# The MLP of a hybrid decoder step: seven products with fewer sums, accumulated onto read PSUM banks, and a reordered end

## The chip, the cores and the metric

The kernel runs on one core of a Trainium2 chip, in one launch. The metric is the time of one execution on the device, in microseconds (us). TensorE multiplies, VectorE and ScalarE read PSUM and work on SBUF, GpSimd works on SBUF alone, SyncE issues most of the transfers.

## The reference

One layer for 1024 prompt tokens and 32 sample tokens (T = 1056 rows together, processed side by side) and a model width of 1024. Two attention branches, merged by gates, come first. The change lies behind them:

```python
def finish_layer(x, o_a, o_b, ga, gb, p_emb, w_oa, w_ob, w_o, g_ffn, w_up, w_down, g_ple, w_ple_gate, w_ple):
    ...
    x = x + (jax.nn.sigmoid(ga) * ya + jax.nn.sigmoid(gb) * yb) @ w_o
    x = x + jnp.square(jax.nn.relu(rms_norm(x, g_ffn) @ w_up)) @ w_down
    x = x + jax.nn.sigmoid(rms_norm(x, g_ple) @ w_ple_gate) * (p_emb @ w_ple)
    return x
```

with `w_up` 1024 x 4096, `w_down` 4096 x 1024, `w_ple_gate` 1024 x 1024, `w_ple` 256 x 1024, all in float32. A final RMSNorm follows.

## The kernel before

**Number format.** Every float32 operand is split into a high half (rounded to the format that TensorE takes at full rate, `fp32r`) and a low half, the difference. A product is made of three matmuls, high x high, high x low and low x high. ScalarE makes high halves by a copy, GpSimd or VectorE the low halves by a subtraction. All activations stand transposed, features on partitions, tokens in columns.

**Stages.** `run_tail` is the part that the change touches. One program per engine is written out by hand; the engines meet at semaphores only, and each works in its own order. First the merge of the branches, then the output projection (`out`, 8 units of 128 output features in 3 chunks of 352 columns), whose results VectorE adds to the residual `x_res` (`take_output_unit`, L2494) and squares for the RMSNorm. Then the MLP, then the gates of the per-layer embedding (`ple`), then the final norm and the output.

**The MLP.** It has NP = 16 iterations of 256 hidden features each. The up projection of an iteration is a 2 x 2 block product: weights w11, w12, w21, w22 (128 features by 512 inputs each) and the residual in four quadrants (512 inputs by 528 columns). Seven products stand for the eight (a Strassen scheme). Their right operands, sums of quadrants of x, are made once in the head (`k_sum`, `k_hi`, `k_lo`, token 0 to 6). Their left operands are made in each iteration: SyncE loads raw quadrants, GpSimd multiplies them by the norm's gain (`scale_quad`), VectorE adds two (`sum_entry`, L2698), ScalarE makes the high half (`high_entry`, L2688), GpSimd the low half (`low_entry`, L2671). There are three slots for such an entry (`e_hi`, `e_lo`, `e_sum` share room); an entry may be written once the product three entries back is done (`wait_slot`). The products m2, m3, m6, m1, m5, m7, m4 (`multiply_product`, L2776 to L2778, 24 matmuls of 264 columns each) go to two PSUM banks each by `BANKS`.
The four results c11 to c22 are put together in SBUF: ScalarE copies the first summand out of PSUM (`first_of`, L2996), VectorE adds the others (`take_back`, L2913) and applies relu and the norm's factor (`finish_quad`, L2881), ScalarE squares and rounds (`square`, L3001 and L3005), VectorE makes the low half (`low_quad`, L2894). They are the hidden activations `a`.
The down projection of the iteration before, d0 to d3 (`multiply_down`, L2801 to L2803, 36 matmuls of 352 columns each, six chunks of six, in banks 4 to 7 by turns), stands between m3 and m6 of iterations 1 to 14. VectorE adds each chunk to `x_res` (`add_down`, L2903), and a chunk may start once the chunk four back is added. The last two down projections, of iterations 14 and 15, follow the last product m4 one after the other.

**The head and the end.** For i = 0 the squares of `x_res` are summed over features (`sum_features`, L3217), GpSimd makes the root, VectorE a diagonal (`make_factors`), TensorE spreads it over the partitions (`spread_products`, L3209), VectorE copies the factors `rstd_bc`. During the last down projection VectorE sums squares again (L2987), ScalarE and GpSimd make the halves `h3` of `x_res` (L3060, L2753). Then `embed_unit`: for unit 0 all gate chunks (L661 to L663), with the sums and factors in between, then the embedding products (L3185 to L3187); for units 1 to 7 by turns. The gate weights are gained and split by GpSimd (`split_ple`, L2759 to L2763), and so are the low halves of `w_ple` (`w_ple_lo`, L2391); VectorE makes `p_lo` (L2444).

## Time and profile before

| | |
|---|---|
| median of 3 runs | 2596.54 us |
| lowest and highest | 1940.65 and 3026.96 us |
| profiled execution | 1940.81 us |
| its span, first to last instruction | 1939.1 us |
| mean granted TensorE clock | 0.99 of full |
| busy: TensorE, VectorE, GpSimd, ScalarE | 95%, 57%, 38%, 34% |

The profile shows one execution, whose time is that of the shortest of the three runs. PE is TensorE, DVE VectorE, ACT ScalarE, POOL GpSimd. In the timeline a row has its start in us, its duration, and in brackets the idle time of the engine before it with what ended that; matmuls overlap, so that the distance of two starts is the cost of one. PEclk is the clock that was granted, as a share of full speed.

### The profile page before, as it was taken

Reading aid. Unit: us, or ns where it says so; the run is one execution under the profiler, and the core shown is the slowest. Engines: PE = TensorE matmul, PEld = TensorE weight load, DVE = VectorE, ACT = ScalarE, POOL = GpSimd, SP = SyncE. Lnnn points to the kernel's source line nnn. Section 1 sums busy time; section 2 is a strip of 40 time slices with the busy share of each in tenths; the row PEclk is TensorE's granted clock in tenths of the full one; section 3 lists DMA queues with packets and bytes.
Section 4 is the critical chain, followed back from the end, with each engine's and each line's share of the span. In section 5 each row is a group of like instructions: output and inputs, shape, how many; then the busy total and the mean of one; then the engine's idle time right before and its main releaser. Section 6 shows DMA issues by size and latency. Waiting matters only on the chain.

```text
span 1939.1 us, 35110 instructions
## 1 busy us (share of the span) xinstructions
PE 1848.8 (95%) x13805; PEld 1704.5 (88%) x13805; DVE 1108.3 (57%) x2198; ACT 652.7 (34%) x1274; POOL 739.8 (38%) x581
## 2 busy tenths in 40 slices
PE   8999999999899998999998899999999999988897
PEld 7977799998766666789998899999999999988897
DVE  5144122223848874875456766666666666677665
ACT  5232123323544444651123323333322222245122
POOL 5323122231514010106565544444444444448641
PEclk9999999999999999999999999999999999999999
DMA  7333285651011127016412222222222322222102
GB/s 237 107 121 129 97 246 172 186 165 56 12 43 44 41 59 221 17 44 201 134 44 82 87 88 96 89 88 88 93 98 94 129 98 88 93 71 93 33 23 90
DMA packets 170268, 193.84 MB, mean 100 GB/s; under 512 B 17530, under 2 KB 142298, under 8 KB 169474
## 3 DMA queue, kind: packets, MB, share of 16 engines
q1 hardware_dynamic: 152866, 161.85, 26.4%
q10 hardware_dynamic: 14816, 28.12, 4.1%
q8 instruction: 105, 1.72, 0.4%
q0 software_dynamic: 2432, 1.74, 0.4%
q14 instruction: 49, 0.40, 0.1%
HBM read 161.13 MB, written 63.97 MB: 116 GB/s over the span
## 4 chain that ended last, share of the span: by engine, by line
PE 45%; DVE 4%; POOL 3%; issue 2%; ACT 1%; DMA 0%; DVEq 0%; ACTq 0%; POOLq 0%
PE bank L2801 6%; PE bank L2802 6%; PE bank L2803 6%; PE bank L661 4%; PE bank L662 4%; PE bank L663 4%; PE bank L2776 4%; PE bank L2778 4%; PE bank L2777 4%; DVE c L2881 1%; POOL e_lo L2671 1%; DVE e_sum L2698 1%; DVE c L2913 1%; ACT e_hi L2688 1%; PE bank L3256 0%
## 5 line engine op out<-in xcount | busy, mean ns | idle before, releaser
L2903 DVE TENSOR_TENSOR x_res<-bank,x_res 128x352 f32<-128x352 f32 x384 | 200.7, 523 | 145.6 <-PE bank L2803 145.5
L2776 PE MATMUL bank<-k_hi,e_hi 128*128 128x264 f32 x896 | 260.3, 291 | 19.5 <-POOL e_lo L2671 16.6
L2777 PE MATMUL bank<-k_lo,e_hi 128*128 128x264 f32 x896 | 256.5, 286 | 0.0
L2778 PE MATMUL bank<-k_hi,e_lo 128*128 128x264 f32 x896 | 256.2, 286 | 0.0
L2801 PE MATMUL bank<-a_hi,e_hi 128*128 128x352 f32 x768 | 249.8, 325 | 3.0 <-DVE x_res L2903 3.0
L2802 PE MATMUL bank<-a_lo,e_hi 128*128 128x352 f32 x768 | 247.2, 322 | 0.0
L2803 PE MATMUL bank<-a_hi,e_lo 128*128 128x352 f32 x768 | 247.2, 322 | 0.0
L2671 POOL TENSOR_TENSOR e_lo<-e_sum,e_hi 128x512 fp32r<-128x512 f32 x80 | 112.5, 1407 | 267.9 <-ACT e_hi L2688 267.9
L2776 PEld LDWEIGHTS bank<-k_hi,e_hi 128*128 128x128 f32 x896 | 170.6, 190 | 24.5 <-issue 17.8
L2671 POOL TENSOR_TENSOR e_lo<-raw,e_hi 128x512 fp32r<-128x512 f32 x96 | 143.0, 1496 | 115.3 <-ACT e_hi L2688 113.8
L2778 PEld LDWEIGHTS bank<-k_hi,e_lo 128*128 128x128 f32 x896 | 170.8, 191 | 0.0
L2777 PEld LDWEIGHTS bank<-k_lo,e_hi 128*128 128x128 f32 x896 | 170.7, 190 | 0.0
L2688 ACT ACTIVATE e_hi<-e_sum 128x512 fp32r<-128x512 f32 x80 | 50.7, 634 | 338.7 <-DVE e_sum L2698 338.7
L2801 PEld LDWEIGHTS bank<-a_hi,e_hi 128*128 128x128 f32 x768 | 144.2, 188 | 6.3 <-DVE x_res L2903 5.7
L2803 PEld LDWEIGHTS bank<-a_hi,e_lo 128*128 128x128 f32 x768 | 144.4, 188 | 0.0
L2802 PEld LDWEIGHTS bank<-a_lo,e_hi 128*128 128x128 f32 x768 | 144.3, 188 | 0.0
L974 DVE TENSOR_TENSOR gt_scaled<-bank,rstd_bc 128x352 f32<-128x352 f32 x48 | 25.1, 524 | 195.7 <-PE bank L663 192.5
L449 PE MATMUL bank<-wn_hi,h_hi 128*128 128x512 f32 (+5 forms) x360 | 132.9, 369 | 0.0
L451 PE MATMUL bank<-wn_hi,h_lo 128*128 128x512 f32 (+5 forms) x360 | 131.0, 364 | 0.0
L450 PE MATMUL bank<-wn_lo,h_hi 128*128 128x512 f32 (+5 forms) x360 | 130.5, 363 | 0.0
L2913 DVE TENSOR_TENSOR c<-c,bank 128x528 f32<-128x528 f32 x128 | 89.7, 701 | 69.3 <-PE bank L2778 33.3
L661 PE MATMUL bank<-h_hi,wu_hi_gates 128*128 128x352 f32 x384 | 128.0, 333 | 0.3 <-PEq L314 0.3
(371 smaller groups left out, 4494.0 us busy)
## 6 DMA issues: line engine op xcount, KB each, us to landing
raw<-in_w_up SPq DMA_DIRECT2D x64, 256.0 KB, 3.2
raw<-in_w_down SPq DMA_DIRECT2D x64, 256.0 KB, 2.6
gate_d<-gate_out ACTq DMA_DIRECT2D x16, 528.0 KB, 3.7
f_gates<-gate_d ACTq DMA_DIRECT2D x24, 352.0 KB, 3.9
w_stage_gates<-in_w_in SPq DMA_DIRECT2D x16, 512.0 KB, 6.9
ws_ring<-in_cache_win_k SPq DMA_DIRECT2D x8, 1024.0 KB, 6.0
ws_ring<-in_cache_win_v SPq DMA_DIRECT2D x8, 1024.0 KB, 6.5
ls_keys<-in_cache_ckv SPq DMA_DIRECT2D x64, 128.0 KB, 2.3
```

Source lines behind the costliest of these rows:

```text
L449: pe.matmul(out, a, w, start=k == 0, stop=False)
L450: pe.matmul(out, a, v, start=False, stop=False)
L451: last = pe.matmul(out, c, w, start=False, stop=k == KD - 1)
L661: pe.matmul(out, w, a, start=n == 0, stop=False)
L2671: pool.tensor_tensor(g.e_lo[s][:, :], src[:, :], g.e_hi[s][:, :].bitcast(F32), ALU.subtract).then_inc(g.e_ready, 1)
L2776: pe.matmul(out, w[:, k], a, start=k == 0, stop=False)
L2777: pe.matmul(out, w[:, k], b, start=False, stop=False)
L2778: last = pe.matmul(out, v[:, k], a, start=False, stop=k == 3)
L2801: pe.matmul(out, w[:, k, unit], a_hi[:, k, cols], start=k == 0, stop=False)
L2802: pe.matmul(out, w[:, k, unit], a_lo[:, k, cols], start=False, stop=False)
L2803: last = pe.matmul(out, v[:, k, unit], a_hi[:, k, cols], start=False, stop=k == 1)
L2903: dve.tensor_tensor(x, g.bank[:, 4 + n % 4, :CH], x, ALU.add).then_inc(g.x_added, 1)
```

## The change

The seven products become those of the variant with fewer sums (Winograd's form), p1 to p7. Four weight sums t1 to t4 are made instead of five, t1, t3 and t4 in place over raw quadrants, t2 in the slot of p6. Products whose results are only ever wanted as a sum are accumulated in PSUM: p6 onto p1's banks, after ScalarE has copied these (c11), then p7 onto the same (after the copy for c21), then p4 (after VectorE's take for c22); p3 onto p5's banks. c12 is finished straight from the banks. In iteration 0 some sums stay in SBUF. The order of products is one list, `ORDER`. In the last iteration d0 stands between p2 and p6; the remaining down products of the last two projections alternate.
In the output projection ScalarE makes the high half of the weights (`high_of_weights`) and GpSimd the low half, where GpSimd made both. Four weight quadrants of iteration 0 and two of iteration 1 are gained by ScalarE (`gain_first`). The loads of `w_ple` and `p_t` are issued right behind the last p4 and those of the gate weights behind the last low quadrant; `w_ple_lo` and `p_lo` are made among the last down products. Unit 0 of the embedding starts with its embedding products, then six of eight parts of its gates, the column sums, and the other two parts.

```diff
 CW = HALF // 2
 NP = FF // (2 * P)
 Q = 4 * P
-SUMS = {"m2": 1, "m6": 2, "m1": 3, "m5": 4, "m7": 5}
-PRODUCTS = ("m2", "m3", "m6", "m1", "m5", "m7", "m4")
+PRODUCTS = ("p1", "p2", "p6", "p5", "p7", "p3", "p4")
 DOWN = ("d0", "d1", "d2", "d3")
-TOKENS = {"m2": 0, "m3": 1, "m6": 2, "m1": 3, "m5": 4, "m7": 5, "m4": 6}
-BANKS = {"m2": 0, "m3": 2, "m6": 0, "m1": 4, "m5": 6, "m7": 0, "m4": 2}
-QUADS = ("c22", "c12", "c11", "c21")
-FIRST = ("c21", "c22", "c12", "c11")
-def entries_of(i):
+TOKENS = {"p1": 0, "p7": 1, "p6": 2, "p3": 3, "p5": 4, "p2": 5, "p4": 6}
+LAST = NP - 1
+C_NAMES = ("c11", "c12", "c21", "c22")
+QUADS = {True: ("c22", "c21", "c12", "c11"), False: ("c11", "c22", "c21", "c12")}
+COPIES = {True: ("c11", "c12", "c21", "c22"), False: ("c11", "c21", "c22")}
+TAKES = {True: ("c21+p3", "c22+p7", "c22+x", "c22f", "c21+p5", "c21f", "c12+x", "c12f", "c11+p2", "c11f"),
+         False: ("c11+p2", "c11f", "c22+x", "c22f", "c21+z", "c21f", "c12f")}
+SUMS = {True: ("t3", "t1", "t2", "t4"), False: ("t1", "t2", "t3", "t4")}
+def program_of_products():
+    order = [(0, name) for name in ("p1", "p7", "p6", "p3", "p5", "p4", "p2")]
+    for i in range(1, LAST):
+        order += [(i, name) for name in PRODUCTS[:2] + DOWN + PRODUCTS[2:]]
+    order += [(LAST, name) for name in PRODUCTS[:2] + ("d0",) + PRODUCTS[2:]]
+    return order + [(LAST, "d1"), (NP, "d0"), (LAST, "d2"), (NP, "d1"), (LAST, "d3"), (NP, "d2"), (NP, "d3")]
...
+def bank_of(i, name):
     if i == 0:
...
+        return {"p1": 0, "p6": 0, "p4": 0, "p7": 2, "p3": 6, "p5": 4, "p2": 6}[name]
+    x = 2 * (i % 2)
+    return {"p1": x, "p6": x, "p7": x, "p4": x, "p2": 2 - x, "p5": 4, "p3": 4}[name]
...
+def sum_weights(dve, g, i, name):
+    product = g.e_sum[slot_of(i, "p6")][:, :]
+    if name == "t1":
+        wait_gained(dve, g, i, "w11")
+        wait_gained(dve, g, i, "w21")
+        if i == 0:
+            dve.wait_ge(g.summed, sums_until(0, "t3"))
+        out, one, other = quad_of(g, i, "w21"), quad_of(g, i, "w21"), quad_of(g, i, "w11")
+    elif name == "t2":
+        wait_gained(dve, g, i, "w22")
+        dve.wait_ge(g.summed, sums_until(i, "t1"))
+        wait_slot(dve, g, i, "p6")
+        out, one, other = product, quad_of(g, i, "w22"), quad_of(g, i, "w21")
+    elif name == "t3" and i == 0:
+        wait_gained(dve, g, i, "w21")
+        wait_gained(dve, g, i, "w22")
+        dve.wait_ge(g.w_split, g.out_step.unit + KD)
+        out, one, other = g.raw[2][:, :], quad_of(g, i, "w22"), quad_of(g, i, "w21")
+    elif name == "t3":
+        dve.wait_ge(g.summed, sums_until(i, "t2"))
+        dve.wait_ge(g.e_ready, ENTRY[i, "p1"] + 1)
+        out, one, other = quad_of(g, i, "w11"), product, quad_of(g, i, "w11")
+    else:
+        wait_gained(dve, g, i, "w12")
+        dve.wait_ge(g.summed, sums_until(i, "t2"))
+        if i:
+            dve.wait_ge(g.e_ready, ENTRY[i, "p2"] + 1)
+        out, one, other = g.raw[3][:, :] if i == 0 else quad_of(g, i, "w12"), quad_of(g, i, "w12"), product
+    dve.tensor_tensor(out, one, other, ALU.subtract).then_inc(g.summed, 1)
...
 def split_last(pool, g, stage, split, at):
-    pool.wait_ge(g.w_loaded[0], (g.steps[-1].turn + 1) * 16)
-    pool.wait_ge(g.e_ready, ENTRY[NP - 1, "m4"] + 1)
-    split_ple(pool, g, stage, split, 0, at + 1)
-    for name in DOWN[:3]:
-        low_entry(pool, g, NP, name)
+    low_entry(pool, g, LAST, "d1")
+    low_entry(pool, g, NP, "d0")
+    pool.wait_ge(g.p_hi_s, 1)
+    for n in range(8):
+        part = (slice(None), n // 4, slice(n % 4 * 256, n % 4 * 256 + 256))
+        done = pool.tensor_tensor(g.wp_lo[part], g.wp[part], g.wp_hi[part].bitcast(F32), ALU.subtract)
+    done.then_inc(g.wp_lo_s, 1)
+    low_entry(pool, g, LAST, "d2")
+    low_entry(pool, g, NP, "d1")
     for n in range(NCH * KD):
         if n == 6:
+            low_entry(pool, g, LAST, "d3")
+            low_entry(pool, g, NP, "d2")
+        if n == 12:
             low_entry(pool, g, NP, "d3")
+            pool.wait_ge(g.w_loaded[0], (g.steps[-1].turn + 1) * 16)
+            split_ple(pool, g, stage, split, 0, at + 1)
         m, c = divmod(n, NCH)
         cols = slice(c * CH, (c + 1) * CH)
         pool.wait_ge(g.h3_hi_s, n + 1)
...
+    s, n, bank = slot_of(i, name), TOKENS[name], bank_of(i, name)
+    onto = name in ("p6", "p4") or (i > 0 and name in ("p7", "p3"))
     w, v = (x[s][:, :].rearrange("p (k c) -> p k c", k=4) for x in (g.e_hi, g.e_lo))
     pe.wait_ge(g.e_ready, ENTRY[i, name] + 1)
     for c in range(2):
         out, cols = g.bank[:, bank + c, :CW], slice(c * CW, (c + 1) * CW)
         for k in range(4):
             a, b = g.k_hi[n][:, k, cols], g.k_lo[n][:, k, cols]
-            pe.matmul(out, w[:, k], a, start=k == 0, stop=False)
-            pe.matmul(out, w[:, k], b, start=False, stop=False)
-            last = pe.matmul(out, v[:, k], a, start=False, stop=k == 3)
+            pe.matmul(out, w[:, k], a, start=k == 0 and not onto, stop=False, skip_group_check=onto)
+            pe.matmul(out, w[:, k], b, start=False, stop=False, skip_group_check=onto)
+            last = pe.matmul(out, v[:, k], a, start=False, stop=k == 3, skip_group_check=onto)
     last.then_inc(g.m_done, 1)
...
+def take(dve, g, i, label):
+    at, name = takes_until(i, label), label[:3]
     c = g.c[name][:, :]
-    dve.wait_ge(g.c_s, 12 * i + at - 1)
-    if i == 0:
-        dve.wait_ge(g.bc_got, 3)
-    dve.scalar_tensor_tensor(c, c, 0.0, g.rstd_bc[:, th * HALF:(th + 1) * HALF], ALU.max, ALU.mult).then_inc(g.c_s, 1)
+    t = int(name[2]) - 1
+    rstd = g.rstd_bc[:, t * HALF:(t + 1) * HALF]
+    if label[3] == "f":
+        if i > 0 and name == "c12":
+            dve.wait_ge(g.m_done, DONE[i, "p4"])
+            dve.wait_ge(g.a_lo_s, quads_until(i - 1, name))
+            dve.scalar_tensor_tensor(halved(c), halves_of(g, bank_of(i, "p4")), 0.0, halved(rstd), ALU.max, ALU.mult).then_inc(g.taken, 1)
+            return
+        dve.wait_ge(g.taken, at - 1)
+        if i == 0:
+            dve.wait_ge(g.bc_got, 3)
+        dve.scalar_tensor_tensor(c, c, 0.0, rstd, ALU.max, ALU.mult).then_inc(g.taken, 1)
+        return
+    product = {"x": {"c12": "p4", "c22": "p6" if i == 0 else "p7"}.get(name), "z": "p3"}.get(label[4:], label[4:])
+    dve.wait_ge(g.m_done, DONE[i, product])
+    dve.wait_ge(g.copied_c, copies_until(i, name))
+    dve.wait_ge(g.taken, at - 1)
+    dve.tensor_tensor(halved(c), halved(c), halves_of(g, bank_of(i, product)), ALU.add).then_inc(g.taken, 1)
...
 def accumulate_mlp(dve, g):
-    def last_quads(i):
-        take_back(dve, g, i, "c11", 2, "m4", 9)
-        finish_quad(dve, g, i, "c11", 10)
-        take_back(dve, g, i, "c21", 2, "m4", 11)
-        finish_quad(dve, g, i, "c21", 12)
-        low_quad(dve, g, i, "c11")
+    low_of_last(dve, g, 2)
+    add_square(dve, g, g.rstd_bc, NCH - 1, NCH * KD)
+    low_of_last(dve, g, 3)
+    low_of_both(dve, g, 1)
+    sum_weights(dve, g, 0, "t4")
+    low_of_both(dve, g, 2)
+    low_of_both(dve, g, 3)
+    copy_feature_sums(dve, g)
+    low_late(dve, g, 6, 0, g.late_lo_dve)
+    low_late(dve, g, 6, 1, g.late_lo_dve)
+    make_factors(dve, g, 0)
...
+    for i in range(1, NP):
+        take(dve, g, i, "c11+p2")
+        take(dve, g, i, "c11f")
+        if i < LAST:
+            add_down(dve, g, i, "d0")
+            sum_weights(dve, g, i, "t1")
+            add_down(dve, g, i, "d1")
+            add_down(dve, g, i, "d2", (0,))
+        else:
+            add_down(dve, g, i, "d0", (0, 1))
+            sum_weights(dve, g, i, "t1")
+        for name in ("t2", "t3", "t4"):
+            sum_weights(dve, g, i, name)
+        if i < LAST:
+            add_down(dve, g, i, "d2", range(1, 6))
+            add_down(dve, g, i, "d3")
+            low_quad(dve, g, i, "c11")
+        else:
+            add_down(dve, g, i, "d0", range(2, 6))
+        take(dve, g, i, "c22+x")
+        take(dve, g, i, "c22f")
+        if i == LAST:
+            low_quad(dve, g, i, "c11")
+        low_quad(dve, g, i, "c22")
+        take(dve, g, i, "c21+z")
+        take(dve, g, i, "c21f")
+        take(dve, g, i, "c12f")
         low_quad(dve, g, i, "c21")
...
     dve.memset(g.rstd_bc[:, :], 0.0).then_inc(g.clear_s, 1)
     dve.memset(g.stat[:, :], float(D)).then_inc(g.stat_s, 1)
-    add_down(dve, g, NP - 1, range(24))
+    add_down(dve, g, LAST, "d1")
     dve.wait_ge(g.clear_s, 2)
     for n in range(NCH * KD):
-        add_down(dve, g, NP, (n,))
-        if n:
+        if n == 6:
+            add_last_square(dve, g, n - 1)
+            dve.wait_ge(g.p_hi_s, 2)
+            dve.tensor_tensor(g.p_lo[:, :, :], g.p_t[:, :, :], g.p_hi[:, :, :].bitcast(F32), ALU.subtract).then_inc(g.p_lo_s, 1)
+            add_down(dve, g, LAST, "d2")
+        if n == 12:
+            add_last_square(dve, g, n - 1)
+            add_down(dve, g, LAST, "d3")
+        add_down(dve, g, NP, f"d{n // 6}", (n % 6,))
+        if n not in (0, 6, 12):
             add_last_square(dve, g, n - 1)
     add_last_square(dve, g, NCH * KD - 1)
...
-    pe.wait_ge(g.w_split, st.unit + m + 1)
     if m == 0:
-        for c in range(NCH):
-            gate(c)
         pe.wait_ge(g.wp_lo_s, 1)
         pe.wait_ge(g.p_lo_s, 1)
         for c in range(NCH):
             embedding(c)
+        pe.wait_ge(g.w_split, st.unit + 1)
+        for c in range(NCH):
+            if c == 2:
+                pe.wait_ge(g.x_added, ENDS_OF_CHUNKS)
+            gate(c, range(6))
+        pe.wait_ge(g.acc_s, 2 * NCH * KD)
+        sum_features(pe, g, g.rstd_bc, 7)
+        for c in range(NCH):
+            gate(c, range(6, KD))
+        spread_products(pe, g, 1, 2, CH)
     else:
+        pe.wait_ge(g.w_split, st.unit + m + 1)
         for c in range(NCH):
             gate(c)
             embedding(c)
```

VectorE in a middle iteration, from the finish of c22 to that of c21, which is the last but for two low halves; before:

```order
L2881 SCALAR_TENSOR_TENSOR c22_12599<-c22_12599,rstd_bc_53 128x528
L2913 TENSOR_TENSOR c12_12597<-c12_12597,bank 128x528
L2881 SCALAR_TENSOR_TENSOR c12_12597<-c12_12597,rstd_bc_53 128x528
L2913 TENSOR_TENSOR c11_12596<-c11_12596,bank 128x528
L2698 TENSOR_TENSOR e_sum1_12611<-raw0_12601,raw1_12602 128x512
L2913 TENSOR_TENSOR c11_12596<-c11_12596,bank 128x528
L2894 TENSOR_TENSOR a_lo_12593<-c22_12599,a_hi_12592 128x528
L2894 TENSOR_TENSOR a_lo_12593<-c12_12597,a_hi_12592 128x528
L2913 TENSOR_TENSOR c11_12596<-c11_12596,bank 128x528
L2881 SCALAR_TENSOR_TENSOR c11_12596<-c11_12596,rstd_bc_53 128x528
L2913 TENSOR_TENSOR c21_12598<-c21_12598,bank 128x528
L2881 SCALAR_TENSOR_TENSOR c21_12598<-c21_12598,rstd_bc_53 128x528
```

and of the changed kernel, from the low half of c11 to the end of the iteration:

```order
L3056 TENSOR_TENSOR a_lo_12593<-c11_12596,a_hi_12592 128x528
L3044 TENSOR_TENSOR c22_12599<-c22_12599,bank 128x528
L3038 SCALAR_TENSOR_TENSOR c22_12599<-c22_12599,rstd_bc_53 128x528
L3056 TENSOR_TENSOR a_lo_12593<-c22_12599,a_hi_12592 128x528
L3044 TENSOR_TENSOR c21_12598<-c21_12598,bank 128x528
L3038 SCALAR_TENSOR_TENSOR c21_12598<-c21_12598,rstd_bc_53 128x528
L3033 SCALAR_TENSOR_TENSOR c12_12597<-bank,rstd_bc_53 128x528
L3056 TENSOR_TENSOR a_lo_12593<-c21_12598,a_hi_12592 128x528
L3056 TENSOR_TENSOR a_lo_12593<-c12_12597,a_hi_12592 128x528
```

The takes of c12 and c11 and the weight sum between them are gone from here, c12 is finished from the bank, and the low half of c22 stands ahead of the take of c21.

GpSimd from the last entries of the down products to the first gate units (`e_lo` are entries, `h3_lo` low halves of the residual, `f_stat` the root); before:

```order
L2671 TENSOR_TENSOR e_lo1_12612<-raw4_12605,e_hi1_12610 128x512
L2759 TENSOR_TENSOR w_stage_ple_12627<-w_stage_ple_12627,gains_52 128x1024
L2761 TENSOR_TENSOR wu_ple_12629<-w_stage_ple_12627,ones_50 128x1024
L2763 TENSOR_TENSOR wu_ple_12629<-w_stage_ple_12627,wu_ple_12629 128x1024
L2671 TENSOR_TENSOR e_lo2_12615<-raw5_12606,e_hi2_12613 128x512
L2671 TENSOR_TENSOR e_lo0_12609<-raw4_12605,e_hi0_12607 128x512
L2671 TENSOR_TENSOR e_lo1_12612<-raw5_12606,e_hi1_12610 128x512
L2753 TENSOR_TENSOR h3_lo_12617<-x_res_12630,h3_hi_12616 128x352 x6
L2671 TENSOR_TENSOR e_lo2_12615<-raw4_12605,e_hi2_12613 128x512
L2753 TENSOR_TENSOR h3_lo_12617<-x_res_12630,h3_hi_12616 128x352 x18
L236 TENSOR_SCALAR f_stat_12565<-f_stat_12565 128x9
L239 TENSOR_TENSOR f_stat_12565<-f_stat_12565,nhalf_51 128x9
```

and of the changed kernel:

```order
L2889 TENSOR_TENSOR w_ple_lo_12623<-w_ple_sb_12622,w_ple_hi_12621 128x256 x8
L2853 TENSOR_TENSOR e_lo1_12612<-raw0_12601,e_hi1_12610 128x512
L2853 TENSOR_TENSOR e_lo2_12615<-raw3_12604,e_hi2_12613 128x512
L2904 TENSOR_TENSOR h3_lo_12617<-x_res_12630,h3_hi_12616 128x352 x6
L2853 TENSOR_TENSOR e_lo0_12609<-raw1_12602,e_hi0_12607 128x512
L2853 TENSOR_TENSOR e_lo1_12612<-raw4_12605,e_hi1_12610 128x512
L2904 TENSOR_TENSOR h3_lo_12617<-x_res_12630,h3_hi_12616 128x352 x6
L2853 TENSOR_TENSOR e_lo2_12615<-raw5_12606,e_hi2_12613 128x512
L2910 TENSOR_TENSOR w_stage_ple_12627<-w_stage_ple_12627,gains_52 128x1024
L2912 TENSOR_TENSOR wu_ple_12629<-w_stage_ple_12627,ones_50 128x1024
L2914 TENSOR_TENSOR wu_ple_12629<-w_stage_ple_12627,wu_ple_12629 128x1024
L2904 TENSOR_TENSOR h3_lo_12617<-x_res_12630,h3_hi_12616 128x352 x12
```

The eight pieces of `w_ple_lo` moved from behind the root to ahead of all `h3_lo`, the split of the first gate unit from ahead of the last projection's entries to ahead of the last twelve `h3_lo`.

## Rows read from the trace of the kernel before

**Rows 1.** The page's busy times (busy us, share of the span, instructions).
```profile
PE 1848.8 (95%) x13805; PEld 1704.5 (88%) x13805; DVE 1108.3 (57%) x2198; ACT 652.7 (34%) x1274; POOL 739.8 (38%) x581
```
**Rows 2.** Stretches of 50 us: busy time of each engine, granted clock, DMA.
```profile
1050.00:1100.00 50.00, 38.46 (x269) 37.41 (x270) 37.32 (x40) 20.36 (x29) 31.29 (x17) 0.93 0.10 32
...
1200.00:1250.00 50.00, 49.54 (x351) 49.26 (x350) 32.22 (x53) 14.34 (x24) 21.06 (x16) 1.00 0.26 87
...
1700.00:1750.00 50.00, 43.76 (x316) 43.04 (x315) 35.27 (x51) 18.65 (x31) 20.02 (x16) 0.97 0.23 72
```
**Rows 3.** TensorE's timeline in the loop (start, us, instruction, idle before it).
```profile
1131.70 0.36 PE L2776 MATMUL bank<-k_hi,e_hi 128*128 128x264 f32 x1 [0.45 <-POOL e_lo L2671]
...
1669.53 0.39 PE L2801 MATMUL bank<-a_hi,e_hi 128*128 128x352 f32 x1
...
1692.56 0.28 PE L2776 MATMUL bank<-k_hi,e_hi 128*128 128x264 f32 x1
...
1707.02 0.28 PE L2778 MATMUL bank<-k_hi,e_lo 128*128 128x264 f32 x1
...
1707.74 0.36 PE L2776 MATMUL bank<-k_hi,e_hi 128*128 128x264 f32 x1 [0.45 <-POOL e_lo L2671]
```
**Rows 4.** TensorE's timeline in the head, from the first product.
```profile
1046.49 0.36 PE L2776 MATMUL bank<-k_hi,e_hi 128*128 128x264 f32 x1 [0.60 <-DVE x_res L2494]
...
1060.78 2.02 PE L3209 MATMUL bank<-f_diag,ones 128*128 128x128 f32 x16 [2.17 <-DVE f_diag L3234]
...
1076.19 0.56 PE L2776 MATMUL bank<-k_hi,e_hi 128*128 128x264 f32 x1 [3.86 <-POOL e_lo L2671]
...
1093.44 0.40 PE L2801 MATMUL bank<-a_hi,e_hi 128*128 128x352 f32 x1
```
**Rows 5.** TensorE's timeline in the last iteration, down products and gates.
```profile
1716.77 0.36 PE L2776 MATMUL bank<-k_hi,e_hi 128*128 128x264 f32 x1 [2.81 <-POOL e_lo L2671]
...
1732.95 0.32 PE L2801 MATMUL bank<-a_hi,e_hi 128*128 128x352 f32 x1
...
1739.92 0.43 PE L2801 MATMUL bank<-a_hi,e_hi 128*128 128x352 f32 x1 [2.98 <-DVE x_res L2903]
...
1789.88 0.63 PE L661 MATMUL bank<-h_hi,wu_ple 128*128 128x352 f32 x1 [5.04 <-issue]
...
1815.12 0.43 PE L661 MATMUL bank<-h_hi,wu_ple 128*128 128x352 f32 x1 [3.59 <-POOL wu_ple L2763]
...
1919.79 2.10 PE L3217 MATMUL bank<-ones,final_total 128*128 128x1 f32 x18 [2.67 <-DVE final_total L3162]
```
**Rows 6.** Stretch of 6 us in the head, columns as in rows 2.
```profile
1066.00:1072.00 6.00, 6.00 (x40) 6.00 (x39) 5.87 (x4) 0.07 (x1) 5.85 (x2) 0.74 0.15 44
```
**Rows 7.** VectorE, ScalarE, GpSimd: groups by shape (busy, mean ns), and single rows.
```profile
L2903 DVE TENSOR_TENSOR x_res<-bank,x_res 128x352 f32<-128x352 f32 x384 | 200.7, 523 | 145.6 <-PE bank L2803 145.5
...
L2913 DVE TENSOR_TENSOR c<-c,bank 128x528 f32<-128x528 f32 x128 | 89.7, 701 | 69.3 <-PE bank L2778 33.3 <-ACT c L2996 31.5
...
L2881 DVE SCALAR_TENSOR_TENSOR c<-c,rstd_bc 128x528 f32<-128x528 f32 x64 | 69.5, 1085 | 2.2
...
L2987 DVE TENSOR_TENSOR rstd_bc<-rstd_bc,h_square 128x352 f32<-128x352 f32 x24 | 20.2, 843 | 0.3 <-ACT h_square L3063 0.2
...
L2688 ACT ACTIVATE e_hi<-e_sum 128x512 fp32r<-128x512 f32 x80 | 50.7, 634 | 338.7 <-DVE e_sum L2698 338.7
...
L2671 POOL TENSOR_TENSOR e_lo<-e_sum,e_hi 128x512 fp32r<-128x512 f32 x80 | 112.5, 1407 | 267.9 <-ACT e_hi L2688 267.9
...
L2763 POOL TENSOR_TENSOR wu_ple<-w_stage_ple,wu_ple 128x1024 fp32r<-128x1024 f32 x8 | 19.5, 2436 | 0.6
...
1717.65 1.75 DVE L2698 TENSOR_TENSOR e_sum<-raw,raw 128x512 f32<-128x512 f32 x1 [2.90 <-POOL raw L2654]
...
1801.44 2.89 DVE L2444 TENSOR_TENSOR p_lo<-p_t_sb,p_hi 128x2112 fp32r<-128x2112 f32 x1
...
1824.72 0.53 DVE L3162 TENSOR_TENSOR final_total<-final_total,tail_square 128x352 f32<-128x352 f32 x1 [0.57 <-ACT tail_square L2481]
```

793 lines of the change are left out of this document (421 added, 372 removed).

## The prediction

> **What bounds the kernel now.** I read the page's busy shares first. TensorE is busy for 1848.8 us of a span of 1939.1 [rows 1], so only the time in which it stands, or runs at half clock, can be won. The stretches of 50 us [rows 2] say where: from 1100 to 1700 us it is saturated (49.5 of 50), and just ahead of that and from 1700 on it loses 6 to 12 us in a stretch. The change touches the program from the output projection (from about 950 us) to the end. So I then read TensorE's own timeline there, stage by stage: what ended each wait, and how long a stage takes beside its bare matmul work.
>
> The bare work comes from one full iteration of the MLP loop. Its four down products (144 matmuls of 352 columns) run from 1669.53 to 1692.56, 23.03 us, 0.160 each; the matmuls of 264 columns that follow start 0.1215 us apart (119 steps from 1692.56 to 1707.02, the last start ahead of the next row) [rows 3]. A product of 24 is 2.92 us, a down product 5.76, an iteration of seven and four 43.4. The loop's period is (1707.74 - 1131.70)/13 = 44.3 us: 0.87 us lost each time, with one visible wait of 0.45 on GpSimd's low half, ahead of m2 [rows 3].
>
> The change has the same number of matmuls, of the same shapes. Accumulation onto a bank that was read replaces a start flag. No row shows that case; the first matmul of a group and the later ones step alike, so I take 0, with 0.12 us a product (one more matmul step) as the upper bound, which over 62 such products is 7.5 us, and no gain below 0, since columns are streamed all the same.
>
> **Part 1, the head (i = 0).** Before, from the first product at 1046.49 to the first down product at 1093.44 is 46.95 us [rows 4], for nine products (26.2), the column sums (2.1, as at the end [rows 5]) and the broadcast of the factors (2.0 and its short third part, 2.4): 30.7. So 16.3 are lost, to waits of 2.17 and 3.86 among others and to a half clock about them [rows 4, 6]; the first row's wait of 0.60 goes on top. Afterwards p1 needs only units 0 to 3 and a weight quadrant that ScalarE gains and rounds early: no wait, +0.6. p7 follows likewise. p6 is what is late next. VectorE must first do, after the last residual add, ten pieces (both, k_sum2, t2, k_sum3, five low halves and squares, t4), since GpSimd's low half of p6 waits for t4, which still reads the place that it overwrites. At 0.70 us a piece [rows 7] that is 7 us from about 1047, then 1.4 for the low half: p6 starts near 1055.5, where TensorE is free at 1045.9 + 5.8 = 1051.7. A new wait of about 4 us. The broadcast before p4 waits for root, diagonal and three takes, while p3 and p5 cover most of it: 0.5. One half-clock spell after the 4 us, 1 us. Left lost: 5.5 of 16.9. Gain 11.4, from 7 (p6 as late as 1058 with contention) to 14 (half of its wait gone).
>
> **Part 2, the fourteen gaps of the loop.** The variant takes five adds of a bank and one weight sum off VectorE (8 to 3 at 0.70, 5 to 4), and one copy off ScalarE. Weight sums are made during the down products, in place, so that the low halves of p5, p7 and p4 no longer wait for a sum at the slot. I followed one iteration by each engine's order, with p4 of the iteration before ending at 0. Slots: each e_hi waits for the product three entries back, then 0.63 (ScalarE) and 1.4 (GpSimd) [rows 7], against 5.8 of cover: met everywhere, by 2 us or more. p6's sum is ready at 21 against a start at 28.9. Three sums in a row delay the additions of the second d2 chunk by 2.1, where four banks allow 2.2. The tight chain is the last one: p4 ends at 0, VectorE takes c12 out of the bank (1.1, so until 1.2 [rows 7]), low half of c21, ScalarE squares and rounds c12, VectorE forms its low half, done between 3.9 and 5.4, and d0 wants it at 5.83, after p1 and p2; p2 wants c12's bank at 2.92 and has it at 1.2. So the gap of 0.87 goes, 14 times: 12.2. Because the chain's slack is down to 0.4 us in the unfavourable order, I take 11. Bounds 3 (0.6 us of overrun each time) and 12.2.
>
> **Part 3, the last iteration and the down products.** Before, the seven products of i = 15 take 1732.95 - 1707.74 = 25.2 for 20.4, with the wait of 2.81 for m6 and a half clock behind it [rows 5]. Now d0 stands between p2 and p6 and covers the sums; p6 still waits for t4 and a low half, about 0.7 to 1.5. Gain 3.5 (2 to 4.5).
> The eight down products take from 1732.95 to 1789.88 - 5.04 = 1784.84, 51.9 us for 46.1: 2.98 for the first additions, and 2.8 because in the last 24 chunks VectorE needs an addition of 0.52 and a square of 0.84 [rows 7], which overlap to some 1.2 a chunk, against TensorE's 0.96. Interleaved, plain additions stand between those with squares, and only the last twelve in a row run behind, within the banks' slack. But p_lo, 128 x 2112 and 2.89 us [rows 7], moves from the broadcast, where nobody waited, into VectorE's queue ahead of d2's additions: the fifth chunk of d2 waits 2 to 3 us. And d1's fifth chunk waits 1.3, because low c12 and a memset stand first. Left 4.4 for 5.8: gain 1.4, from -2 (the two embedding loads land late, ScalarE stands ahead of the squares) to +4.
>
> **Part 4, from the last chunk to the second gate unit.** Before, 1815.12 - 1784.84 = 30.3 us. The gates wait 5.04 for the last low halves, and GpSimd, in order root, eight w_ple_lo pieces, three steps of split, holds the second unit until 1815.12 [rows 5]. Now the embedding products (2.9) and six eighths of the gates (8.6) come first, and w_ple_lo is made among the down products. GpSimd's split of unit 0 (about 6.5 us, 2.4 its longest step [rows 7]) stands ahead of the last twelve low halves, so these end about 6.5 us after the last chunk, still under the 11.5 of TensorE's work. Then column sums (13.6 after the last chunk), root (16), split of unit 1 (22.5): the second unit starts at 22.6 to 23.5. Gain 7.3, of which 0.8 goes into a half-clock spell: 6.5 (4 to 8).
>
> What stays at nothing: ScalarE makes the high half of w_o where GpSimd did: 0.63 us for 512 columns [rows 7], so about 1.2 for 1024, once in a unit of three chunks of 24 matmuls (11.5 us at the step above), and GpSimd's load falls. If it were late, each unit would cost its excess. The tail's 2.67 ahead of the column sums stays.
>
> **The sum.** 11.4 + 11 + 3.5 + 1.4 + 6.5 = 33.8. Against the profiled execution's 1940.8 us (span 1939.1 plus 1.7) that is 1907; 1 us for what I have overlooked gives 1908. The median of the three runs shown is 2596.5, their lowest is 1940.65, and the profile agrees with the lowest: the rows say nothing of what made the other two long, so my time is for runs like the profiled one.
>
> **A rule against the change.** Squares that take 0.53 us alone take 0.84 beside GpSimd's work [rows 7]. By the Trainium skill (SBUF — State Buffer, Who interferes with whom), a VectorE instruction with two SBUF inputs contends with a GpSimd instruction that reads SBUF; with one input from PSUM it doesn't. On that the trace agrees. What the change removes are mostly adds from a bank, which the rule leaves alone, and what it keeps at the end of each iteration are low halves with two SBUF inputs; that is rival 3.
>
> **Rivals.**
> 1. Everything fits, no new wait: p6's 4 us, d2's and the spells go too. 1908 - 4 - 1 - 3 - 2 = 1898. For it: slots have slack. Against: t4's place in the queue is fixed, and so is p_lo's. Chance 0.12.
> 2. Head and end give back what they win (another half-clock spell or two, ScalarE's gains in four small pieces a quadrant slower than thought, wp and p_t landing late): 11 + 11 of gains left, 1919. For it: before, the waits of the head stood beside a granted clock of 0.74 on average over 6 us, a mix of 2.4 and 1.2 GHz [rows 6], and the waits of the end had such spells too. Chance 0.24. The Trainium skill (TensorE: Matmul & The Clock Gate, What's actually happening) knows the two levels, full and half, that this row averages.
> 3. The rule above, as a mechanism of this loop: GpSimd's low half of d0 and its two gains fall on the low halves of c21 and c12 (a two-input subtraction of 0.7 took 1.75 beside a gain [rows 7]), d0 waits about 1 us each time, and the loop wins nothing: 1908 + 11 + 1 = 1920, to 1930. Chance 0.12.
> 4. Slower: the same chain, but in earnest. VectorE's order puts take c21, its finish and c12's behind low c22, which waits for ScalarE's rounding, which stands behind the rounding of p1, which waits for a slot. If that costs one hand-over more, c12 is ready at 9 instead of 5.4. From 2.4 us of overrun (34/14) it decides the sign: 3.4 us gives 1908 + 11 + 48 = 1967; over 2% it takes 5. For it: nothing else in the loop has so little slack. Against: before, VectorE had the longer chain at the same place and d0 started without a wait [rows 4]. Chance 0.05.
> That matmuls onto a read bank cost a step each (+8, 1916) has 0.03, within 2. The forecast itself, 1902 to 1915, has 0.44.
>
> **Chances.** The limit of 2% (about what a measurement of this kernel tells from no change) lies at 1902. Faster by more: rival 1, and 0.07 of the forecast's low end, 0.19. Slower by more than 2%: most of rival 4, 0.04. Within: 0.77. The range holds the forecast, all but the last of rival 1, and 2 and 3: 1897 to 1931.
>
> **What would show it.** Per iteration: a period of 43.4 to 43.6, no wait on e_lo ahead of the first product, d0 without a wait on a_lo. In the head: p6 waiting 3 to 5 us for its low half, the first down product 35 to 37 us after p1. In the end: a wait of x_res inside d2 of about 2, no wait of 5 after the last chunk, and the second gate unit 23 us after it, released by the split. I am wrong if the period is above 44.3, or if TensorE waits for bank takes (c11, c22, c12) between products.

## The result: 1.3% faster, two thirds of what was forecast

The changed kernel takes 1918.0 us (1917.85 to 1918.64, four executions); its profiled execution took 1917.9 us, with a span of 1916.2. The ratio to the kernel before is 0.987, interval 0.985 to 0.990; it is made with the executions of before that agree with its profiled one (1940.65 and 1945.53), not with the two long ones, of which no row says why they were long. By the profiles 22.9 us were won (1940.8 to 1917.9), where 32.8 were forecast.

The page of the changed kernel has, for [rows 1]:
```profile
PE 1840.3 (96%) x13805; PEld 1701.3 (89%) x13805; DVE 1017.6 (53%) x2111; ACT 659.3 (34%) x1296; POOL 715.5 (37%) x568
```
VectorE has 91 us less to do, and TensorE's busy time fell by 8.5, though it has the same matmuls: a matmul at half clock is busy for longer, so busy time holds lost time too. The same stretches as in [rows 2], and four short ones on the clock (engines' busy times, then the granted clock, DMA share, GB/s):
```profile
1050.00:1100.00 50.00, 43.99 (x300) 43.44 (x299) 36.55 (x48) 22.50 (x40) 29.88 (x18) 0.90 0.36 126
1200.00:1250.00 50.00, 50.00 (x369) 50.00 (x368) 25.09 (x42) 16.34 (x27) 23.35 (x18) 1.00 0.29 96
1700.00:1750.00 50.00, 44.21 (x290) 43.05 (x289) 34.23 (x52) 24.84 (x44) 34.87 (x32) 0.97 0.28 91
1050.00:1055.00 5.00, 0.42 (x3) 0.26 (x2) 4.91 (x7) 5.00 (x9) 1.99 (x2) 0.78 0.00 0
1055.00:1060.00 5.00, 5.00 (x26) 5.00 (x26) 0.19 (x1) 0.56 (x1) 2.57 (x2) 0.54 0.38 106
1890.00:1895.00 5.00, 0.57 (x4) 0.28 (x2) 2.84 (x8) 1.49 (x3) 0.00 (x0) 0.75 0.00 0
1895.00:1899.00 4.00, 3.93 (x19) 3.90 (x20) 0.40 (x4) 0.00 (x0) 0.00 (x0) 0.50 0.00 0
```
The loop is full now (50.00 of 50, 49.54 before). TensorE's timeline, the rows that answer to [rows 3 to 5]:
```profile
1044.19 0.28 PE L2928 MATMUL bank<-k_hi,e_hi 128*128 128x264 f32 x1
...
1054.77 0.56 PE L2928 MATMUL bank<-k_hi,e_hi 128*128 128x264 f32 x1 [4.58 <-POOL e_lo L2853]
...
1070.94 2.05 PE L3419 MATMUL bank<-f_diag,ones 128*128 128x128 f32 x16 [1.43 <-DVE c L3044]
...
1085.03 0.32 PE L2953 MATMUL bank<-a_hi,e_hi 128*128 128x352 f32 x1
...
1648.94 0.32 PE L2953 MATMUL bank<-a_hi,e_hi 128*128 128x352 f32 x1
...
1699.27 0.36 PE L2928 MATMUL bank<-k_hi,e_hi 128*128 128x264 f32 x1 [1.02 <-POOL e_lo L2853]
...
1719.28 0.43 PE L2953 MATMUL bank<-a_hi,e_hi 128*128 128x352 f32 x1 [1.32 <-DVE x_res L3066]
...
1728.90 0.43 PE L2953 MATMUL bank<-a_hi,e_hi 128*128 128x352 f32 x1 [1.69 <-POOL e_lo L2853]
...
1735.47 0.66 PE L2953 MATMUL bank<-a_hi,e_hi 128*128 128x352 f32 x1 [2.47 <-DVE x_res L3066]
...
1763.93 0.32 PE L3387 MATMUL bank<-p_hi,w_ple_hi 128*128 128x352 f32 x1
...
1788.21 0.40 PE L3372 MATMUL bank<-h_hi,wu_ple 128*128 128x352 f32 x1 [1.18 <-DVE ple_tmp L3344]
...
1895.07 3.77 PE L3429 MATMUL bank<-ones,final_total 128*128 128x1 f32 x18 [4.50 <-DVE final_total L3357]
```
Between these marks the two kernels can be compared stage by stage. The first product starts at 1044.19 for 1046.49 [rows 4]; the last chunk ends at 1764.10 and the last embedding product at 1890.57, in the kernel before at 1784.84 and 1917.11.

| stage | before | after | won | forecast |
|---|---|---|---|---|
| up to the first product | 1046.49 | 1044.19 | 2.3 (1.7 of it ahead of the changed code) | 0.6 |
| first product to first down product | 46.95 | 40.84 | 6.1 | 10.8 |
| to the fourteenth iteration's d0 (13 periods) | 576.1 | 563.9 | 12.2 | 10.2 |
| from there to the last chunk's end | 115.3 | 115.2 | 0.15 | 5.7 |
| to the second gate unit | 30.3 | 24.1 | 6.2 | 7.3 |
| from there to the last product | 102.0 | 102.4 | -0.4 | -0.8 |
| to the span's end | 22.0 | 25.6 | -3.6 | 0 |

(The forecast's 11 for fourteen gaps is divided 10.2 and 0.8; 1 us was set aside besides.) Three stages miss: the head by 4.7, the down products by 5.5, the end by 3.6. From here on "the head" is the stretch from the first product to the first down product, and "the down products" are those from d1 of the last iteration to the last chunk.

The unaltered kernel, run again, took 1920.1 us (1918.3 to 1921.5), and the kernel before 1938 to 1948 over all groups. Where few microseconds matter, the stages of the trace are therefore compared, in which the same code repeats thus: the head 40.2 to 41.5 us (in one profile 42.5), the down products 48.7 to 50.2.

### The profile page after: what moved, and what is told of

Its sections match the earlier page's. It is cut to its first block and busy times, and to the rows that moved or that the text cites. A ratio compares the mean times of both kernels' runs of the same rounds, so it can differ in the third digit from the quotient of the medians.

```text
span 1916.2 us, 35091 instructions
## 1 busy us (share of the span) xinstructions
PE 1840.3 (96%) x13805; PEld 1701.3 (89%) x13805; DVE 1017.6 (53%) x2111; ACT 659.3 (34%) x1296; POOL 715.5 (37%) x568
## 5 line engine op out<-in xcount | busy, mean ns | idle before, releaser
L2853 POOL TENSOR_TENSOR e_lo<-raw,e_hi 128x512 fp32r<-128x512 f32 x160 | 225.9, 1416 | 263.4 <-ACT e_hi L2843 263.4
L3066 DVE TENSOR_TENSOR x_res<-bank,x_res 128x352 f32<-128x352 f32 x384 | 196.7, 521 | 108.3 <-PE bank L2955 106.5
L2843 ACT ACTIVATE e_hi<-raw 128x512 fp32r<-128x512 f32 x160 | 100.2, 627 | 231.5 <-PE bank L2955 173.2
L664 PE MATMUL bank<-h_hi,wu_lo_gates 128*128 128x352 f32 x384 | 123.5, 322 | 0.0
L663 PE MATMUL bank<-h_lo,wu_hi_gates 128*128 128x352 f32 x384 | 123.2, 321 | 0.0
```

The lines of the kernel that those rows point to most:

```text
L2853: pool.tensor_tensor(g.e_lo[s][:, :], source_of(g, i, name), g.e_hi[s][:, :].bitcast(F32), ALU.subtract).then_inc(g.e_ready, 1)
L3066: dve.tensor_tensor(x, g.bank[:, 4 + n % 4, :CH], x, ALU.add).then_inc(g.x_added, 1)
```

## The experiments

All edits are made to the changed kernel. k5 and k6 are the right operands of p2 and of p4.

**1. t4 early.**
```diff
         sum_weights(dve, g, 0, "t2")
+        sum_weights(dve, g, 0, "t4")
         low_of_both(dve, g, 0)
...
     low_of_both(dve, g, 1)
-    sum_weights(dve, g, 0, "t4")
```


> VectorE forms t4 directly behind t2, ahead of four low halves, instead of behind them; nothing else changes. Theory A (the head was mis-sized by what stands behind p6's wait): the low half of p6 is ready some 3.5 us earlier, so p6 waits about 1 us instead of 4.58, and the half clock behind the wait (p6's 24 matmuls take 5.34 us for 2.9) goes too: the stretch from p1 to the first down product falls from 40.84 to about 35 us, the time from 1917.9 to 1912. Rival B (the head is bound by the chain of the factors, column sums to diagonal, which starts when its inputs are ready and not when TensorE gets there): the stretch stays within 1 us of 40.84, since the wait ahead of the broadcast grows by what p6 wins.

1916.5 us; the head takes 39.85.
```profile
1052.37 0.56 PE L2929 MATMUL bank<-k_hi,e_hi 128*128 128x264 f32 x1 [2.35 <-DVE k_lo L2646]
...
1068.22 2.92 PE L3419 MATMUL bank<-f_diag,ones 128*128 128x128 f32 x16 [1.89 <-DVE c L3045]
```
p6 waits half as long and ends 3.0 us earlier, and 1.0 us is left, the number of rival B, just outside the spread. Its mechanism holds only in part: the wait ahead of the broadcast grew by 0.5. The other 1.5 us went behind this wait, where the broadcast's first part takes 2.92 for 2.05 us (granted clock 0.70 from 1068 to 1071).

**2. Fillers.**
```diff
             elif name == "p6":
+                fill(pe, 32, g.bank[:, 6, :CW], g.k_hi[0][:, 0, :P], g.k_hi[0][:, 0, :CW])
...
 def write_products(pe, g):
+    fill(pe, 24, g.bank[:, 6, :CH], g.wp_hi[:, 0, :P], g.p_hi[:, 0, :CH])
```


> TensorE gets work that computes nothing needed: 32 matmuls of 264 columns ahead of p6 in the head, 24 of 352 columns ahead of the last column sums, both into a bank that nobody reads; they end before the waits do. Theory A (what these waits cost is the wait plus a spell at half clock behind it): the waits for p6's low half and for the last squares end when they did, but p6 takes 3.0 us instead of 5.34 and the last column sums 2.1 instead of 3.77: 2.3 us won in the head and about 2 at the end, 1913.5. Of the 7.64 us of p3 and p5 nothing is won, because the broadcast behind them waits for the diagonal: that wait grows from 1.43 to about 3.2. Rival B (these rows are long for another reason, the arrival of their operands or their small shape): their lengths stay, 1917.9.

1915.0 us; the head takes 38.68, from the last product to the end 23.9 with the fillers for 25.6. Here the timeline, then the clock in the stretches of p6, of p3 and of the last fillers and sums:
```profile
1056.01 0.36 PE L2928 MATMUL bank<-k_hi,e_hi 128*128 128x264 f32 x1 [0.76 <-POOL e_lo L2853]
...
1070.01 2.05 PE L3426 MATMUL bank<-f_diag,ones 128*128 128x128 f32 x16 [1.45 <-DVE c L3051]
...
1894.08 2.10 PE L3436 MATMUL bank<-ones,final_total 128*128 128x1 f32 x18 [0.70 <-DVE final_total L3364]
```
```profile
1056.00:1059.00 3.00, 2.99 (x24) 3.00 (x25) 0.43 (x1) 0.79 (x1) 2.83 (x2) 1.00 0.09 19
...
1061.00:1064.00 3.00, 3.00 (x18) 3.00 (x19) 2.94 (x4) 1.28 (x2) 2.82 (x3) 0.66 0.36 101
...
1893.00:1896.00 3.00, 2.30 (x20) 1.99 (x19) 0.86 (x3) 0.47 (x1) 0.00 (x0) 1.00 0.00 0
```
Theory A holds for p6 (3.15 us for 5.34) and for the sums (2.10 for 3.77): a wait of 4.5 us costs about 2 us more behind it. One detail is wrong: p3 and p5 still take 7.64, for the clock falls again behind the column sums, though TensorE had no idle time between these and p6.

**3 and 4. The two waits in the down products.**
```diff
+    low_entry(pool, g, LAST, "d2")
+    low_entry(pool, g, NP, "d1")
     pool.wait_ge(g.p_hi_s, 1)
     for n in range(8):
...
-    low_entry(pool, g, LAST, "d2")
-    low_entry(pool, g, NP, "d1")
```


> GpSimd makes the low halves of the last iteration's d2 and of the sixteenth's d1 ahead of the eight pieces of w_ple_lo instead of behind them. Theory A (the eight pieces, 6.2 us, are what the third of the last down products waits for, 1.69 us, but VectorE is the later one behind it): the wait of 1.69 goes, and the wait for VectorE's additions behind p_lo, 2.47, grows by nearly as much; the time is 1917.5 (1916.5 to 1918). Rival B (TensorE is bound by that wait alone): 1.7 us less, 1916.2 or below.


```diff
-            dve.tensor_tensor(g.p_lo[:, :, :], g.p_t[:, :, :], ..., ALU.subtract).then_inc(g.p_lo_s, 1)
-            add_down(dve, g, LAST, "d2")
+            for q in range(6):
+                add_down(dve, g, LAST, "d2", (q,))
+                part = (slice(None), q // 3, slice(q % 3 * CH, (q % 3 + 1) * CH))
+                done = dve.tensor_tensor(g.p_lo[part], g.p_t[part], ..., ALU.subtract)
+            done.then_inc(g.p_lo_s, 1)
```


> p_lo is formed on VectorE in six pieces of 352 columns, one behind each addition of the last iteration's d2, instead of in one piece of 2112 ahead of them. Theory A (the one piece costs TensorE its wait and a spell at half clock behind it): the wait of 2.47 goes, and the 72 matmuls behind it take 11.6 us for 13.3: about 4 us less, 1914. Rival B (VectorE is the bound of the whole stretch, so that p_lo costs its 3 us wherever it stands): the wait is spread over several chunks and the time stays at 1917 to 1918.

1919.5 (1916.5 to 1918 was expected) and 1917.8 us; the down products take 49.8 and 49.3, inside the spread of the unaltered code. Waits of the first, then VectorE's timeline in the second:
```profile
1736.14 0.43 PE L2953 MATMUL bank<-a_hi,e_hi 128*128 128x352 f32 x1 [3.32 <-DVE x_res L3066]
...
1760.73 0.43 PE L2953 MATMUL bank<-a_hi,e_hi 128*128 128x352 f32 x1 [1.40 <-DVE x_res L3066]
```
```profile
1735.60 0.51 DVE L3066 TENSOR_TENSOR x_res<-bank,x_res 128x352 f32<-128x352 f32 x1
1736.03 0.82 DVE L3135 TENSOR_TENSOR p_lo<-p_t_sb,p_hi 128x352 fp32r<-128x352 f32 x1
```
The wait that each edit was aimed at is gone, and others on VectorE's additions have taken its place: theory A of the one, rival B of the other. A piece of p_lo takes 0.82, so that with an addition a chunk takes VectorE 1.2 us, for TensorE's 0.96.

**5. Gains on ScalarE.**
```diff
-        dve.tensor_scalar(x, x, g.gains[:, 3, ...], None, ALU.mult).then_inc(g.pdone_s, 1)
...
                     act.activation(g.sq[:, :].unsqueeze(1), chunk_of(g.x, i, q), ACT.Square).then_inc(g.sq_s, 1)
+                    x = chunk_of(g.x, i, q)
+                    act.activation(x, x, ACT.Copy, scale=g.gains[:, 3, ...]).then_inc(g.pdone_s, 1)
```


> In the embedding stage ScalarE multiplies a chunk of x by its gains, behind its own square, instead of VectorE. Theory A (the longer wait ahead of the last column sums, 4.50 for 2.67, comes from VectorE's lag: it takes each chunk 6 to 8 us behind TensorE where it was 4 to 5.5, is stopped beside GpSimd's split once in a unit and so never catches up before the splits end): with 0.31 us less a chunk, and the multiplication that took 2.53 beside the split gone, VectorE catches up with TensorE inside the stage, takes the last chunk 0.3 to 0.4 us behind its last gate matmul instead of 2.20, the wait is 2.7 or less, and the half clock on the sums (3.77) shrinks too: 1915 (1914 to 1916). Rival B (the wait is set by the fixed chain from the last chunk to its square): nothing but about 0.3 us moves.

1915.8 us. In the changed kernel VectorE's timeline has, once in a unit, beside GpSimd's split (1833.42 to 1840.12):
```profile
1836.45 1.40 DVE L3357 TENSOR_TENSOR final_total<-final_total,tail_square 128x352 f32<-128x352 f32 x1 [0.73 <-ACT tail_square L2506]
1837.78 2.53 DVE L3351 TENSOR_SCALAR x_res<-x_res,gains  x1
...
1891.49 0.52 DVE L3344 TENSOR_TENSOR ple_tmp<-bank,rstd_bc 128x352 f32<-128x352 f32 x1
```
and the last sums of this experiment, with VectorE's last take ahead of them:
```profile
1887.89 0.52 DVE L3346 TENSOR_TENSOR ple_tmp<-bank,rstd_bc 128x352 f32<-128x352 f32 x1 [1.23 <-PE bank L3375]
```
```profile
1891.48 2.78 PE L3430 MATMUL bank<-ones,final_total 128*128 128x1 f32 x18 [2.67 <-DVE final_total L3358]
```
Theory A: VectorE now waits for TensorE's chunk (1.23) instead of following it late, the wait is 2.67 as before the change, and from the last product to the end it is 22.9 us for 25.6. The multiplication, 0.40 us elsewhere, takes 2.53 beside the split and ends at 1840.31, just behind the split's last instruction, which had started first (1837.56 to 1840.12). By the Trainium skill (SBUF — State Buffer, Who interferes with whom), a `tensor_scalar` can enter a two-port mode, and of such an instruction and one of GpSimd the one issued first has the shared ports for its whole length, while the other is blocked. The trace agrees; that the multiplication ran in this mode no row shows.

**6. Gates first again.**
```diff
-        for c in range(NCH):
-            embedding(c)
...
+        for c in range(NCH):
+            gate(c)
+            if c == 0:
+                pe.wait_ge(g.acc_s, 2 * NCH * KD)
+                sum_features(pe, g, g.rstd_bc, 7)
+        spread_products(pe, g, 1, 2, CH)
...
+        for c in range(NCH):
+            embedding(c)
```


> The first unit of the embedding stage in the old order: three whole gates, column sums behind the first, broadcast, then the three embedding products; all else as changed, w_ple_lo and the splits on GpSimd too. Forecast's view (Part 4's 6.5 us come from two sources, work that TensorE has before the last low halves are needed, and the splits that are done earlier): the wait of 5 to 6 us comes back behind the last chunk, but the second unit, which then waits for broadcast and takes more than for its split, starts about 27 us after the last chunk instead of 24.1: 1921. Rival (all of the 6.2 us is the order of TensorE's work): 30.3 us again, 1924. Other rival (all of it is GpSimd's order): 24.5, 1918.

1919.3 us. The wait is back,
```profile
1769.67 0.63 PE L3372 MATMUL bank<-h_hi,wu_ple 128*128 128x352 f32 x1 [5.21 <-POOL h_lo L2904]
```
but the broadcast ends at 1787.55 and the second unit starts some 2.9 us later, 26 us after the last chunk (1764.46), and from the last chunk to the span's end it is 152.7 us for 152.1. So TensorE's order is worth 2 us of the 6.2 at the second unit and 0.6 at the end; the rest came from GpSimd's order.

**7. Slack of the loop.**
```diff
         low_quad(dve, g, i, "c21")
+        if i < LAST:
+            for _ in range(3):
...
+                dve.tensor_tensor(spare, g.rstd_bc[:, :HALF], g.rstd_bc[:, HALF:], ALU.subtract).then_inc(g.spare_s, 1)
...
         low_quad(dve, g, i, "c12")
```


> VectorE does three needless subtractions of 528 columns (0.7 us each, 2.1 in all) in each of the loop's fourteen iterations, just ahead of the low half of c12, the last link of the chain that d0 waits for. By the prediction's slack of 0.4 us d0 waits 1.7 us each time: 24 us, 1942. By the trace of the changed kernel (low half of c12 done at 1126.30, d0 starts at 1128.38) the slack is 2.1 us and d0 starts as before: 1918 to 1919.

1975.0 us, and neither number held. The period is 47.36 us for 43.38, with a wait of 2.46 ahead of d0 in each. VectorE's rows, and the stretch behind one of these waits:
```profile
1174.87 4.73 DVE L3128 TENSOR_TENSOR h_square<-rstd_bc 128x528 f32<-128x528 f32 x3
1179.53 1.76 DVE L3057 TENSOR_TENSOR a_lo<-c,a_hi 128x528 fp32r<-128x528 f32 x1
...
1181.00:1184.00 3.00, 2.61 (x9) 2.64 (x10) 2.43 (x4) 0.65 (x1) 1.43 (x1) 0.56 0.38 115
```
The three took 4.73 us, not 2.1, since here they stand beside GpSimd's gains, and c12's low half 1.76 for 0.71: 5.8 more. VectorE had stood for 1.0 us ahead of this low half and stands there no more, so it ends 4.6 us later (1181.29), and d0, which starts 0.1 behind it, waits 2.46. That is a slack of some 2.1 us, as the trace of the changed kernel had it, and not the prediction's 0.4. The rest of the 4.0 us by which the period grew is the clock (0.56 in the stretch shown): in most iterations the 144 matmuls behind the wait take 24.8 us for 23.1. And work of 0.7 us put there costs 1.6.

**8 and 9. The chain of the factors.** 8 has both edits, 9 only the first.
```diff
             inverse_root(pool, ...)
+        if ORDER[n][1] == "p2":
             for half in range(2):
                 low_late(pool, g, 5, half, g.late_lo_pool)
...
-    low_late(dve, g, 6, 0, g.late_lo_dve)
-    low_late(dve, g, 6, 1, g.late_lo_dve)
     make_factors(dve, g, 0)
     for label in ("c21+p3", "c22+p7", "c22+x"):
         take(dve, g, 0, label)
+    low_late(dve, g, 6, 0, g.late_lo_dve)
+    low_late(dve, g, 6, 1, g.late_lo_dve)
```


> In the head nothing runs beside the chain of the factors: VectorE makes the two low halves of k6 behind the diagonal and the three takes instead of ahead of it, GpSimd the two of k5 behind the low half of p2. Theory A (the prediction took half a microsecond for this chain, and it costs 3.1: from the end of the column sums to the start of the broadcast it is 9.0 us, because the root takes 3.8 us for 2.0 and the diagonal 3.6 for 1.9 beside other work, while p3 and p5 cover 5.8 to 7.6): the chain falls to about 5.5 us and no longer ends the wait; p4 starts some 2 us earlier, the stretch from p1 to the first down product is 38.5 to 39.5 for 40.84, the time 1916. Rival B (what is moved is needed just behind): p4 or p2 waits for the low halves instead, and the stretch stays within 0.5 us.

1920.8 us; the head takes 45.9 (8: VectorE's timeline, then TensorE's).
```profile
1065.66 1.36 DVE L3446 TENSOR_TENSOR f_diag<-ident,f_stat 128x1152 f32<-128x1152 f32 x1 [2.67 <-POOL f_stat L240]
...
1072.52 5.11 DVE L2572 TENSOR_TENSOR k_lo<-x_res,k_hi 128x1056 fp32r<-128x1056 f32 x2
```
```profile
1077.73 0.56 PE L2929 MATMUL bank<-k_hi,e_hi 128*128 128x264 f32 x1 [5.29 <-issue]
```
The chain is as short as theory A had it (the diagonal takes 1.36 us for 3.62, and the broadcast doesn't wait), but the low halves moved behind it meet GpSimd's and take 5.11 us for 2.79, and p4, which starts 0.1 us behind their end (1077.63), waits for them: rival B in kind, but the head is 5 us longer, where it said 0.5 at most.

> Of the edit that lost 5 us only GpSimd's half: the two low halves of k5 go behind the low half of p2, VectorE keeps its order. Theory A (beside these two, the diagonal takes 3.6 us instead of 1.4 to 1.9, and that is what the broadcast waits for at the end): the chain from column sums to broadcast falls from 9.0 to 7.6 us at most, the wait of 1.43 goes, p2 gets its low halves in time, and the stretch from p1 to the first down product is 39.4 for 40.84. Rival B (they collide with the next thing instead, the low halves of p2 and p1 or VectorE's takes): the stretch is 40.8 or longer.

1916.2 us; the head takes 39.68, 1.3 less than the unaltered kernel of its group and 0.5 below the spread.
```profile
1074.25 0.39 PE L2929 MATMUL bank<-k_hi,e_hi 128*128 128x264 f32 x1 [0.21 <-DVE c L3045]
```
Theory A: the diagonal again takes 1.36, from the column sums to the broadcast it is 7.4 us for 9.0, no wait is left ahead of the broadcast, and 0.21 behind it.

**10 to 12. The unaltered kernel, and the edits together.** (10 is the run told of above; 11 has edits 2 to 5, with 14 fillers at the end; 12 has these, 1 and 9, with 16 fillers in the head.)

> Together: fillers (32 matmuls ahead of p6, 14 ahead of the last column sums), low halves of d2 and d1 ahead of w_ple_lo, p_lo in six pieces, gains on ScalarE. If the effects add up, by the stages measured one by one: head 2.2, down products 0.4 + 0.9 and up to 1.5 more, because the one wait no longer only takes the place of the other, embedding stage and end 3.1 + 0.7: 7.3 to 8.8 us less than the changed kernel beside it. If VectorE bounds the stretch of the down products whatever stands in it, the part from the middle is 1.3 or less and the whole 6 to 7.

> The same with 16 fillers in the head, t4 directly behind t2, and the two low halves of k5 behind the low half of p2. If the factor chain is what held back the gain of the early t4 (1.0 of 3.0 us was left), shortening it lets both through: the stretch from p1 to the first down product is 36 to 37.5 us for 40.84, the whole 9 to 11 us less than the changed kernel. If another piece of VectorE's or GpSimd's queue is late next, the stretch stays above 38.5, and the time is that of the kernel before in this group.

| | time | ratio to before, interval | head | down products | last chunk to end |
|---|---|---|---|---|---|
| 10 | 1920.1 | 0.989, 0.987 to 0.990 | 41.0 | 50.2 | 152.1 |
| 11 | 1912.2 | 0.985, 0.984 to 0.987 | 38.7 | 50.0 | 146.5 |
| 12 | 1910.9 | 0.984, 0.983 to 0.985 | 36.6 | 49.3 | 148.9 |

12 is the fastest kernel here, 9.2 us under the unaltered one of its group. Its head is as short as expected (36.6 for 36 to 37.5), but not for the reason expected. The broadcast waits as before, and from the column sums to it 9.1 us pass:
```profile
1053.24 0.36 PE L2932 MATMUL bank<-k_hi,e_hi 128*128 128x264 f32 x1 [0.47 <-DVE k_lo L2648]
...
1067.32 2.05 PE L3431 MATMUL bank<-f_diag,ones 128*128 128x128 f32 x16 [1.50 <-DVE c L3055]
```
With t4 early, moving the low halves of k5 didn't shorten the chain. What 12 has over the changed kernel is that p6 starts 2.2 us sooner behind the first product (early t4) and takes 3.17 us for 5.34 (fillers). In experiment 1 half of what the early t4 won was lost again to the clock behind the broadcast's wait; here the broadcast takes 2.05. In the down products next to nothing moved (0.2 us of 11's 7.9), as the theory had it by which VectorE bounds the stretch "whatever stands in it".

**13 to 16. What bounds the down products.** Edits 3 and 4 (14 and 16: 3 only) are the base. In 13 and 16 the eight subtractions on GpSimd give way to the first line, in 14 and 16 the subtraction of p_lo to the second, in 15 the last twelve additions of squares to the third, in 16 all 24.
```diff
+            act.activation(g.wp_lo[:, :, :], g.wp[:, :, :], ACT.Copy).then_inc(g.wp_lo_s, 1)
...
+            act.activation(g.p_lo[:, :, :], g.p_t[:, :, :], ACT.Copy).then_inc(g.p_lo_s, 1)
...
+        dve.tensor_tensor(g.rstd_bc[:, one], g.rstd_bc[:, one], g.sq2[:, n % 2, :1], ALU.add).then_inc(g.acc_s, 1)
```


> On the version with the low halves of d2 and d1 first and p_lo in six pieces (its down products alone took 50.04 us from the second of them to the last chunk, the changed kernel's 50.2). Left out: the subtraction of w_ple_lo, which is a copy by ScalarE here, so that the second term of the embedding is wrong. GpSimd is free of 6.2 us beside VectorE's squares. Theory A (what bounds this stretch is VectorE held up beside GpSimd): 48 us or less. Rival B (the sum of VectorE's own work): 49.5 or more. Rival C (TensorE's waits for single events, which these edits already took away one by one): no change, 50.

> Low halves of d2 and d1 first; left out: the subtraction of p_lo, a copy by ScalarE here. VectorE has 3.1 us less to do, 5 less than in pieces. Theory A (held up beside GpSimd): 48.5, since only p_lo's share goes. Rival B (VectorE's own work): 47. If p_lo cost what the forecast said, its wait of 2.5 goes from 49.8: 47.3.

> Low halves first, p_lo in pieces; left out: of the last twelve squares only the first column is added, so the factors of the last stage are wrong. VectorE has about 0.75 us less for each of the last twelve chunks, where it takes 1.19 a chunk against TensorE's 0.96. If the last stretch is what VectorE loses: its 2 us go, 48.0 for 50.04. If the loss is made before it and the banks' slack absorbs the rest: 49.5.

> Left out together: the subtractions of p_lo and w_ple_lo (copies by ScalarE) and of all 24 squares all but the first column. Bare, the seven down products take 40.3 us; what stays are the wait of 1.3 for the first additions and whatever is not VectorE's or GpSimd's doing. If VectorE with GpSimd beside it is the whole cause: 42 to 43. If half a clock or late weights hold it anyway: 45 or more.

Each ran once: 1914.7, 1917.5, 1916.4 and 1913.8 us. The stretch takes 48.8, 46.5, 47.8 and 42.0 us; 48.8 lies between theory A and rival B of 13, and the others are near what was expected of VectorE as the bound (47, 48.0, 42 to 43). In 16 one wait is left, and behind it 228 matmuls run without one:
```profile
1723.15 0.43 PE L2948 MATMUL bank<-a_hi,e_hi 128*128 128x352 f32 x1 [1.32 <-DVE x_res L3061]
```
So VectorE is the bound: its own work most (p_lo 3.2 us, half the squares 1.5 to 2.2), GpSimd beside it by 0.5 to 1.2, the clock only through the waits. 13 and 15 lie inside or near the spread and would prove nothing alone; 14 and 16 lie well outside.

## Why the prediction was right in its order and wrong in its size

The measured 1918 lies in the stated range of 1897 to 1931, but outside the forecast itself (1902 to 1915). What failed are terms priced too low, in three places. In Part 1 it is the half clock behind p6's wait and the chain of the factors (1 and 0.5 us said, 2.4 and 3.2 measured). In Part 3 it is the step by which the down products lose only single waits (4.4 said, 9.9 measured, since VectorE's whole work bounds them). And the end of the kernel, said to stay as it was, lost 3.6. That the sum is no further off is partly luck: the loop gave 2 us more than was said.

**Part 1, the head, 6.7 for 11.4.** p6 started at 1054.77 (1055.5 said) after a wait of 4.58 (4), released by the low half that stands behind t4: right. Two terms failed. "One half-clock spell after the 4 us, 1 us": p6 alone lost 2.4 (5.34 for 2.9), shown by the fillers. And "p3 and p5 cover most of it: 0.5": from column sums to broadcast it is 9.0 us (1061.95 to 1070.94) against a cover of 5.84, 3.2 us. I had priced root and diagonal as they ran before, and not with the low halves of k5 and k6 that the change puts beside them; experiments 8 and 9 show that it is these, and 9 that those of k5 alone are enough. Where p3 and p5 ran at half clock it cost nothing, since they ran inside this chain: in the profile of experiment 3, whose head is unaltered, they took 6.11 us for 7.64, and from the column sums to the broadcast it was still 9.0.

**Part 2, the loop, 13 for 11.** The period is 43.38 us, without a wait anywhere: the bare matmul work, to 0.1. So accumulation onto a bank that was read costs nothing here. That the gap of 0.87 was VectorE's and GpSimd's sums fits, but which of them it was no run shows. The slack was sized too small (0.4 for 2.1), which only cost the prediction its last microsecond.

**Part 3, 0.15 for 5.7 (with one gap of the loop).** 3a was right: p6 waited 1.02 (0.7 to 1.5), and the seven products and d0 lost 1.2 us where the seven lost 4.8. The waits of 3b came as forecast, d1's fifth chunk 1.32 (1.3) and d2's fifth 2.47 (2 to 3), plus one of 1.69 that was only in the bounds: GpSimd's eight pieces of w_ple_lo,
```profile
1721.14 6.20 POOL L2889 TENSOR_TENSOR w_ple_lo<-w_ple_sb,w_ple_hi 128x256 fp32r<-128x256 f32 x8 [7.86 <-ACT w_ple_hi L3242]
...
1719.14 1.92 ACT L3242 ACTIVATE w_ple_hi<-w_ple_sb 128x2048 fp32r<-128x2048 f32 x1 [2.21 <-DMA w_ple_sb<-in_w_ple]
```
ahead of d2's low half. GpSimd had stood idle for 7.86 us before them, for ScalarE's high half, which waited for the load of `w_ple`: "the two embedding loads land late" was what the prediction's lower bound was for. What failed is the step "only the last twelve in a row run behind, within the banks' slack", and with it the way of counting: I added up single waits (4.4 us), where VectorE's work bounds the stretch as a whole. It lost 9.9 (50.2 for 40.3), 8.2 of which went in experiment 16.

**Part 4, 5.8 for 6.5.** 24.1 us to the second unit for 22.6 to 23.5, right in size; but the unit was released by VectorE's first take behind the broadcast, not by the split. Where the broadcast ran faster (2.6 us in experiments 3 and 9, 3.6 here) it was the split, and the unit started 23.1 us behind the last chunk, as forecast. And two thirds of the gain is GpSimd's order, not TensorE's.

**What "stays" did not.** "The tail's 2.67 ahead of the column sums stays": it became 4.50, plus 1.7 of half clock on the sums. The embedding stage starts earlier against VectorE, which takes its chunks 6.2 to 8.2 us behind the start of TensorE's last gate matmul of the chunk, where it was 4.0 to 5.5. Once in a unit GpSimd's split holds VectorE for some 3 us, so that three chunks take it 14.3 us, as TensorE; it can gain on TensorE only behind the last split, 1 us a chunk, and ends 2.20 us behind for 0.35. 4.50 is 2.67 plus this difference. Experiment 5 shows the place, experiment 2 the price of the clock.

**The rivals.** Nearest in time is rival 2 (1919, chance 0.24), in part by luck: head, down products and end gave back 14 us of what they were to win, but the head kept 6 and the loop gave 13. They lost it by the clock and the late load of `w_ple`, as it said, and by GpSimd and VectorE side by side, which it did not. Rival 3, this contention at the end of each loop iteration, did not come where it was looked for: VectorE has 2 us of slack there. It came in the head, in the down products and in the embedding stage.

## What to carry to other kernels

When a change removes waits, find each stretch's total of work for the engine that comes next (here VectorE, with its two-input instructions priced as they run beside GpSimd), and compare it with TensorE's before adding up single waits; where the total is larger, waits only change places. Work that a change moves has a price at its new place, for itself and for its neighbour. And a stage that the change does not touch can still pay, if a follower enters it with more lag and has no slack to catch up.

## What the runs showed of the hardware

TensorE's clock fell also where it had no idle time: 1 to 2 us behind 18 matmuls of one column (2.0 us) it was granted 0.66 on average over 3 us, a mix of both levels, in the run with fillers (1061 to 1064), and p3 and p5 took 7.6 us for 5.8 in all runs but two (6.1). The same wait of 2.47 in the same code was followed by 72 matmuls in 11.75 us in the profiles of experiments 5 to 8, which ran as one group, and in 13.3 in all others; that alone is the spread of the down products. In experiment 3 a wait of 3.32 cost nothing behind it (granted clock 1.00 from 1736 to 1744). What decides was not tried.
